# Splitting the expert weights in pairs: one subtraction of 2048 columns, and six buffers for the high halves

## The reference

```python
lg = xt @ wg + bg;  gsel = argmax(lg)            # group of a token
le_sel = (xt @ we + be)[gsel];  topv, topi = top_k(le_sel, 2)
gates = one_hot(...) * softmax(topv) * p_sel
hu = einsum('td,edf->tef', xt, w_gate_up)         # 2048 -> 2 x 512 for each expert
hg, hv = split(hu, 2)
act = silu(hg) * hv * gates
out = einsum('tef,efd->td', act, w_down)          # 512 -> 2048
x = layer_norm(ALPHA * x + out)
```

## Time and profile before

| | |
|---|---|
| median of 3 runs | 1775.57 us (1772.4 to 1776.09) |
| profiled execution | 1773.6 us, its span 1771.8 us |
| busy share of the span | TensorE 93%, VectorE 79%, ScalarE 64%, GpSimd 3% |
| mean granted TensorE clock | 0.961 of full speed |
| mean DMA rate | 275 GB/s over the span, 351 to 388 GB/s in most slices with windows |

### The profile page before, as it was taken

How to read it: one execution, slowest core, us unless ns; L and a number is a source line. 1 busy time by engine, 2 the same in 40 slices (tenths; PEclk the granted TensorE clock), 3 DMA queues, 4 the chain that set the end, 5 groups by cost and what they waited for, 6 DMA issues and landing times.

```text
span 1771.8 us, 21823 instructions
## 1 busy us (share of the span) xinstructions
PE 1641.6 (93%) x8184; PEld 1230.4 (69%) x8184; DVE 1391.2 (79%) x1738; ACT 1137.0 (64%) x1290; POOL 44.7 (3%) x34
## 2 busy tenths in 40 slices
PE   5999997997999999999999959899998999999995
PEld 5999996985766666666666737566665665665664
DVE  4667675536879988988998926676898899899887
ACT  3465655335667878777777721565776777777674
POOL 0000000000000000000000000000001002001000
PEclk8999998998999999999999969998999999999998
DMA  9555537542869999999999744466998999999990
GB/s 281 155 167 155 167 96 237 176 158 73 318 259 382 353 351 385 354 349 366 385 366 333 291 163 144 150 249 240 388 349 331 349 381 338 346 385 331 333 372 14
DMA packets 146420, 488.11 MB, mean 275 GB/s; under 512 B 5325, under 2 KB 59277, under 8 KB 126893
## 3 DMA queue, kind: packets, MB, share of 16 engines
q1 hardware_dynamic: 141328, 463.75, 71.7%
q0 software_dynamic: 2464, 13.37, 2.5%
q10 hardware_dynamic: 2522, 9.59, 1.6%
HBM read 476.15 MB, written 14.47 MB: 277 GB/s over the span
## 4 chain that ended last, share of the span: by engine, by line
PE 76%; DVE 13%; issue 4%; ACT 3%; DMA 2%; ACTq 1%; DVEq 0%; POOL 0%; POOLq 0%
PE ps L1026 17%; PE ps L1028 17%; PE ps L1027 16%; DVE ring_lo L1460 6%; PE ps L849 4%; PE ps L851 4%; PE ps L850 4%; PE ps L879 2%; PE ps L881 2%; PE ps L880 2%; PE ps L1074 2%; PE ps L861 2%; PE ps L941 1%; DVE xtok L1418 1%; ACT whi L717 1%
## 5 line engine op out<-in xcount | busy, mean ns | idle before, releaser
L1460 DVE TENSOR_TENSOR ring_lo<-ring,whi 128x1024 fp32r<-128x1024 f32 x768 | 922.3, 1221 | 114.1 <-ACT whi L717 106.9
L717 ACT ACTIVATE whi<-ring 128x1024 fp32r<-128x1024 f32 x768 | 806.2, 1060 | 254.7 <-PE ps L1028 247.5
L1026 PE MATMUL ps<-whi,operands 128*96 128x512 f32 x1536 | 624.5, 407 | 35.4 <-issue 17.8
L1028 PE MATMUL ps<-ring_lo,operands 128*96 128x512 f32 x1536 | 609.9, 397 | 0.0
L1027 PE MATMUL ps<-whi,operands 128*96 128x512 f32 x1536 | 608.4, 396 | 0.0
L1026 PEld LDWEIGHTS ps<-whi,operands 128*96 128x96 f32 x1536 | 250.4, 163 | 169.2 <-DVE ring_lo L1460 40.4
L1028 PEld LDWEIGHTS ps<-ring_lo,operands 128*96 128x96 f32 x1536 | 250.8, 163 | 112.1
L1027 PEld LDWEIGHTS ps<-whi,operands 128*96 128x96 f32 x1536 | 252.5, 164 | 99.7
L578 ACT ACTIVATE whi<-ring 128x1024 fp32r<-128x1024 f32 x96 | 100.9, 1058 | 157.4 <-PE ps L851 97.9
L1155 DVE TENSOR_TENSOR ring_lo<-ring,whi 128x1024 fp32r<-128x1024 f32 x96 | 116.2, 1223 | 80.8 <-ACT whi L578 80.6
L849 PE MATMUL ps<-operands,whi 128*128 128x288 f32 x512 | 154.6, 302 | 9.1 <-ACT mark L589 9.1
(11 more groups left out here) (270 smaller groups left out, 1125.3 us busy)
## 6 DMA issues: line engine op xcount, KB each, us to landing
ring<-in_moe_w_gate_up SPq DMA_DIRECT2D x128, 2048.0 KB, 9.2
ring<-in_moe_w_down SPq DMA_DIRECT2D x64, 2048.0 KB, 9.6
ring<-in_lru_w_in SPq DMA_DIRECT2D x16, 2048.0 KB, 10.2
ring<-in_lru_w_out SPq DMA_DIRECT2D x8, 2048.0 KB, 8.8
x_rows<-xtok ACTq DMA_DIRECT2D x4, 1024.0 KB, 4.3
ring<-in_pool_w SPq DMA_DIRECT2D x4, 1024.0 KB, 5.2
xtok<-in_x_prompt SPq DMA_DIRECT2D x2, 1024.0 KB, 8.0
ring<-in_lru_w_a SPq DMA_DIRECT2D x8, 256.0 KB, 5.8
```

Of the source, the lines that this page charges most:

```text
L717: eng.activation(whi[:, i % NPART, :], ring_at(n)[:, at * PART:(at + 1) * PART], ACT.Copy)\
L1026: mm(o, hi, whi[:, i % NPART, cols], start=start, stop=False)
L1028: last = mm(o, hi, lo_at(base + i // PARTS_CHUNK, i % PARTS_CHUNK)[:, cols], start=False, stop=stop)
L1460: TT_(lo_at(n, at), ring_at(n)[:, at * PART:(at + 1) * PART], whi[:, i % NPART, :].bitcast(F32), ALU.subtract).then_inc(lo_ready, 1)
```

## The change

In the windows, VectorE forms the low halves of two parts in one subtraction of 2048 columns, at even i; it waits until the high halves of both exist, and counts `lo_ready` up by two. The high halves get two more buffers, which use the third tile of `xtok` (idle while windows run, once its rows have been stored; hence the wait on `x_out`). ScalarE may now be six parts ahead of TensorE. All tables of what stands at which i (above) stay as they are.

```diff
+NHI = 6
...
+        with nc.sbuf_tensor("whi_more", [128, 3, D], F32R) as whi_more:
+            pass
         xtok = sb("xtok", [128, 3, D])
...
-        def lo_at(n, at):
-            return ring_lo[:, slot_of(n), at * PART:(at + 1) * PART]
+        def lo_at(n, at, parts=1):
+            return ring_lo[:, slot_of(n), at * PART:(at + parts) * PART]
+
+        def whi_at(i, parts=1):
+
+            b = i % NHI
+            if b < NPART:
+                return whi[:, b:b + parts, :].rearrange("p a c -> p (a c)")
+            return whi_more[:, 2, (b - NPART) * PART:(b - NPART + parts) * PART]
...
-                        eng.wait_ge(parts_used, seq * PARTS_WIN + (parts0 - NPART + i + 1))
-                        eng.activation(whi[:, i % NPART, :], ring_at(n)[:, at * PART:(at + 1) * PART], ACT.Copy)\
+                        if first and i in (NPART, NPART + 1):
+                            eng.wait_ge(x_out[l], 48)
+                        if first and l == 0 and i < NHI:
+                            eng.wait_ge(parts_used, parts0 + min(i - NPART, -1) + 1)
+                        else:
+                            eng.wait_ge(parts_used, seq * PARTS_WIN + (parts0 - NHI + i + 1))
+                        eng.activation(whi_at(i), ring_at(n)[:, at * PART:(at + 1) * PART], ACT.Copy)\
                            .then_inc(hi_ready, 1)
...
-                            mm(o, hi, whi[:, i % NPART, cols], start=start, stop=False)
-                            mm(o, lo, whi[:, i % NPART, cols], start=False, stop=False)
+                            mm(o, hi, whi_at(i)[:, cols], start=start, stop=False)
+                            mm(o, lo, whi_at(i)[:, cols], start=False, stop=False)
...
-                        eng.wait_ge(hi_ready, seq * PARTS_WIN + (parts_base(l) + i + 1))
-                        TT_(lo_at(n, at), ring_at(n)[:, at * PART:(at + 1) * PART],
-                            whi[:, i % NPART, :].bitcast(F32), ALU.subtract).then_inc(lo_ready, 1)
+                        eng.wait_ge(hi_ready, seq * PARTS_WIN + (parts_base(l) + i + 2))
+                        TT_(lo_at(n, at, 2), ring_at(n)[:, at * PART:(at + 2) * PART],
+                            whi_at(i, 2).bitcast(F32), ALU.subtract).then_inc(lo_ready, 2)
...
-                        low_part(i)
+                        if i % 2 == 0:
+                            low_part(i)
```

## The result

| | before | after |
|---|---|---|
| median | 1775.56 us (1772.4 to 1776.09) | 1901.29 us (1900.82 to 1903.15) |
| span of the profiled execution | 1771.8 us | 1900.0 us |
| mean granted TensorE clock | 0.961 | 0.954 |
| repeat of a window, layer 1 / layer 2 | 143.3 / 146.8 us | 160.2 to 160.5 / 160.8 to 160.9 us |

What follows compares the result with a forecast made beforehand. TensorE, busy 93% of the span, was taken as the bound, so only its stalls count. Terms summed to 118 us over eight windows, on 1773.6 giving 1891.6, median 1894; own range 1870 to 1915, 8 in 10 within 1862 to 1934.

Steps and rivals of the forecast that it cites:

- (a): TensorE's gated wait at part 32: gating of expert 1 comes behind pair (34,35); cost 2.95 us a window.
- (c): Activation split after each expert delays the odd part's `high`: TensorE waits 1.29 us at expert 1, 0.77 at the others.
- (d): Next rows' splits, parts 88 to 95: pairs delay TensorE by 1.38, 0.95 and 0.43 us; sum 3.2 a window.
- (b): Tanh and gating of experts 0, 2 and 3: the pair comes late, stalls of 1.33 and 0.51 us.
- the clock's: TensorE's clock fall behind part 32: already paid, longer stall need not cost more; taken as nothing, other bound 48 us.
- (e): Head of a window: net +1.35 us in layer 1; +1.4 in layer 2 for head and expert 0 together.
- (f): First windows: layer 1's row splits behind pair (2,3) cost +1.9 us once; layer 2's late routing takes 0.9 off (a).
- The signs: Expected trace: pairs about 2.28 us, VectorE 50 to 60 less busy, 5.4 idle before part 32, layer 1 repeat about 159.
- R1: TensorE's clock also falls in the clusters of stalls: up to 166 us lost, so 1942; chance 14%.
- R2: Faster, as VectorE's saved time counts if the odd `high` is always early: 1772, or 1735; chance 5%.
- R3: Only (a) costs, 24 us, the rest being hidden by 1.96 us of cover and fast catching up: 1800; chance 5%.
- R4: No change: (a) alone remains and the head gives it back; chance 2%.

Runs made afterwards that it cites:

- Experiment 1: The changed kernel with six buffers kept but one subtraction for each part instead of pairs: 1765.44 us, ratio 0.9953 to the kernel before.
- experiment 7: The changed kernel, pairs kept, with tanh and gating, activation split and next-row splits all moved to even places: 1773.62 us, ratio 0.9997 to the kernel before.
- experiment 3: The changed kernel with VectorE gating expert 1 ahead of pair (34, 35), ScalarE's order as it was: 1867.79 us, ratio 1.0539 to the kernel before.
- experiment 5: The changed kernel with the activation's split moved to an expert's end + 8 (even) from end + 7: 1869.8 us, ratio 1.0538 to the kernel before.
- experiment 6: The changed kernel with the next rows' four splits two each at parts 92 and 94, not one each at 91 to 94: 1885.41 us, ratio 1.0629.
- experiment 4: The changed kernel with tanh and gating moved to an expert's end + 4 (even) from end + 3: 1830.64 us, ratio 1.0324 to the kernel before.
- experiment 2: The changed kernel with pairs kept but four high-half buffers instead of six: 2008.97 us, ratio 1.1339 to the kernel before.

## Why the prediction was right

**The mechanism** was as written: a pair needs the `high` of its odd part, and on ScalarE that stands behind work that waits for the whole expert. Experiment 1 shows that the buffers have no share in the loss, experiment 7 that the order has 128 of the 136 us that the pairs cost over experiment 1, and experiments 3, 5 and 6 show (a), (c) and (d) one at a time, each in the parts where the sum had put it; (b) is in what experiment 4 has over experiment 3. That the sum came within 10 us is in part luck: misses of both signs met in it, and the largest, the clock's, was a term that the sum put at nothing.

**(a)** The stall grew by 3.0 us a window, 2.95 forecast. (Its times 5.43, 7.63 and 4.77 take off 0.08 where one subtraction follows another, as in the earlier trace rows, without a word on it.) "That fall is paid already, and the longer stall in (a) need not pay more" is the step that failed: the granted clock was at the lower level for 6.8 us around the end of the longer stall (665.3 to 672.1 in the window shown) and for 3.4 around that of the shorter one (642.1 to 645.5), so part 33 took 2.56 us and not 1.64. In the first window the kernel before had no fall at part 32 at all. Over the eight windows the idle time ahead of part 32 grew by 23.3 us, 22.7 forecast, and the other 8.0 of the 31.3 are the clock's, from 0.3 us in the last window to 2.3 in the first. Experiment 3 took both away together.

**(b), (c)** 1.26 and 0.67 of idle time at expert 0 for 1.33 and 0.77; at expert 1's split 1.37 for 1.29. Experts 0 (in layer 1), 2 and 3 came out 0.3 above the forecast each. Idle time is not what the sum adds up: by the starts of the parts the first stall is 1.43, and the part behind it takes another 0.08. So at expert 2 the stalls of after sum to 2.94 for 2.61, while today's loss, 0.53, was rightly put at 0.5; at expert 3 they are 3.20 for 2.61, and today's loss was 0.35 where the prediction had none.

**(d)** 3.2 for 3.2 over all, with the first stall 1.29 for 1.38.

**(e)** was mis-sized: +0.4 to +0.7 in layer 1 for +1.35, mostly because pair (12,13) was not late (the table load), and in layer 2 head and expert 0 together +0.4 to +0.7 for +1.4, the head by itself 0.1 to 0.4 faster. Why layer 2 missed was not tested, and it is 2.7 of the 3.8 us by which heads and expert 0 came out below the sum, against (a)'s 8.6 above it.

**(f)** +1.5 for +1.9 at the first window. Its deduction of 0.9 for layer 2's first window was right for the wait: the idle time ahead of part 32 grew there from 3.32 to 5.58, by 2.3 for 2.1. Parts 31 to 35 grew by 3.4, and the other 1.2 is the clock again.

**The signs.** The pair's length was 2.287 us for 2.28, the idle time before part 32 5.44 for about 5.4, the repeat in layer 1 160.2 to 160.5 for about 159; VectorE was busy 49 us less, a little under the 50 to 60 forecast. The Trainium skill (VectorE: DVE Perf Modes, "The TRN2 errata") gives a formula by which 2048 columns take 2.29; the trace agrees. It advises tiles of at least 512 elements, so that the fixed cost amortises; the parts of 1024 were past that already. The trace agrees that fewer operations cost VectorE less, 46 us in these subtractions, and the kernel lost 126 all the same.

**The rivals.** R1: no stall of a cluster brought the clock down; the low stretches stand behind the gated wait and where the kernel before had them. The Trainium skill (TensorE: Matmul & The Clock Gate, "Why this matters for your kernels") warns of idle gaps between bursts, but only of gaps longer than any in the clusters, so it does not speak for R1. The trace agrees for the clusters (no fall with three stalls of 0.7 to 1.3 us within some 12 us) and for the stall of 5.44; it goes further than the page at the stalls of 2.4 to 2.5, shorter than those that the page names, where the clock fell in six of seven windows of the kernel before. R2 asked that the odd `high` be early, which held in undisturbed parts alone. R3's 24 us is close to the 23.3 that (a) costs by order alone, but the rest was not hidden. R4's "no change" came only when experiment 7 changed the order.

**The sum.** Forecast 118, measured 128.2 in span. Over all eight windows: (a) 31.3 us for 22.7, +8.6; expert 1's split 11.0 for 10.3, +0.7; expert 2 19.3 for 16.8, +2.5; expert 3 22.8 for 20.8, +2.0; next rows -0.2; heads with expert 0 15.9 for 19.7, -3.8; (f)'s start -0.4; parts without a term +0.9. That is 10.3.

## What to carry to other kernels

Merging two operations moves the need of the first half behind everything that stands before the second half's producer. So look in each producer's stream for what is interposed between the two halves, and put it at the boundaries of the merged unit; deeper buffers cure a lack of space, not an order. Ask of the engine that gets shorter whether anyone waits for it: here VectorE's saved time was worth nothing that shows, and single subtractions with the six buffers were still 8 us faster than well-placed pairs. And read for each long stall which data the waiting instruction truly needs: one count in one wait was worth 31 us, and buffers and order around it, over the kernel before, 9.

## What the runs showed of the hardware

- Around the end of a stall of 5.4 to 5.6 us TensorE's granted clock was at the lower level, 1.2 GHz, for 6.8 us in all eight windows of the changed kernel, 3.5 to 5.5 of them behind the stall. With four buffers (experiment 2) stalls of the same length had 6.8 in six windows and 3.4 in two. Around stalls of 2.4 to 3.3 us in the kernel before it was 3.4 us in seven windows, and in the eighth the clock did not fall.
- Behind stalls of 2.2 to 2.4 us it fell in seven windows of eight in experiment 3 and in four of eight in experiment 7, for 3.4 us each. So at this length the stall alone does not decide.
- Stalls of 0.73, 1.29 and 0.81 us within 12.2 us (parts 86, 90 and 92, changed kernel) left it at the upper level, 2.4 GHz, and so did 1.26, 1.58 and 1.02 within 15 us at a head of layer 2.
- A stall costs more than its idle time: behind an idle time of 1.26 us part 18 started 1.43 late, and part 19 lost another 0.08.
- ScalarE's table load (1.28 us) ran ahead of the data its activation waits for: it ended 1.66 us before that activation began.
- Two subtractions of 1024 columns in a row take 2.36 us, one of 2048 takes 2.29. Merging saves 0.07 us per pair where they stand back to back.
